# Softmax sums divided out in the output norm, and keys and queries squared from PSUM and normed at their one eviction

## What is computed

```python
k_sh = rms_norm((hk @ w_k).reshape(b, s, 8, 2, 64), k_norm_g)      # hk, h: normed residual stream
v_sh = (hk @ w_v).reshape(b, s, 8, 128)
q = rms_norm((h @ w_q[j]).reshape(b, s, 8, 2, 64), q_norm_g[j])
...
probs = softmax(where(causal, q . k * 64**-0.5, -1e30))            # two components per head
diff = probs[:, :, 0] - lam * probs[:, :, 1]
out = diff @ v                                                     # (queries, head, 128)
o = rms_norm(out, subln_g[j]) * (1.0 - lam_init)
x = x + o.reshape(b, s, 1024) @ w_o[j]
```

## Time and profile before

| | |
|---|---|
| time, median of 3 runs | 1270.95 us (1270.5 to 1271.31) |
| the profiled execution: its own time | 1270.56 us |
| its span from first to last instruction | 1268.7 us |
| mean granted TensorE clock over the span | 0.982 |
| TensorE, VectorE, ScalarE, GpSimd busy | 96%, 67%, 43%, 9% of the span |

### The profile page before, as it was taken

The page is one execution under the profiler, slowest core; times in us unless marked ns, Lnnn a source line. Parts: engine busy times, 40 slices in busy tenths (PEclk is TensorE's granted clock), DMA queues, the critical chain, the costliest instruction groups (busy, mean ns, idle before and its releaser), DMA issues.

```text
span 1268.7 us, 16583 instructions
## 1 busy us (share of the span) xinstructions
PE 1213.7 (96%) x6085; PEld 1014.2 (80%) x6085; DVE 843.9 (67%) x1158; ACT 542.1 (43%) x942; POOL 111.8 (9%) x99
## 2 busy tenths in 40 slices
PE   6998997999999999999998989987999999999999
PEld 4787765888888888887998989865888888888887
DVE  7999946577626763676677777664677537762673
ACT  6246966444313441344454545442544324431441
POOL 4000000200000000001234141301200000000000
PEclk9999998999999999999999999997999999999999
DMA  5221001323322223123221211211322322332222
GB/s 214 75 94 64 1 1 36 103 95 99 100 100 99 93 95 111 66 83 116 71 98 34 67 37 64 67 34 34 100 95 88 116 71 95 99 113 87 100 74 92
DMA packets 16615, 104.00 MB, mean 82 GB/s; under 512 B 1840, under 2 KB 1968, under 8 KB 5424
## 3 DMA queue, kind: packets, MB, share of 16 engines
q1 hardware_dynamic: 16560, 103.25, 24.5%
HBM read 101.15 MB, written 2.10 MB: 81 GB/s over the span
## 4 chain that ended last, share of the span: by engine, by line
PE 84%; DVE 10%; ACT 3%; POOL 1%; issue 1%; DMA 0%; SPq 0%; POOLq 0%; DVEq 0%; ACTq 0%
PE bank L1036 67%; PE bank L1154 7%; PE bank L1090 5%; PE bank L1219 2%; DVE prob L982 1%; DVE w_lo L709 1%; DVE small L972 1%; ACT prob L663 1%; DVE w_lo L701 1%; DVE prob L984 1%; POOL sq_sum L417 1%; DVE dT_lo L964 1%; PE bank L1107 1%; ACT w_hi L472 1%; PE bank L1188 1%
## 5 line engine op out<-in xcount | busy, mean ns | idle before, releaser
L1036 PE MATMUL bank<-xg_hi,w_hi 128*128 128x512 f32 x832 | 327.1, 393 | 13.3 <-DVE xg_lo L717 10.9
L1036 PE MATMUL bank<-xg_lo,w_hi 128*128 128x512 f32 x832 | 325.2, 391 | 0.0
L1036 PE MATMUL bank<-xg_hi,w_lo 128*128 128x512 f32 x832 | 325.0, 391 | 0.0
L472 ACT ACTIVATE w_hi<-w_raw 128x2048 fp32r<-128x2048 f32 x83 | 158.3, 1907 | 151.0 <-PE bank L1036 151.0
L701 DVE TENSOR_TENSOR w_lo<-w_raw,w_hi 128x2048 fp32r<-128x2048 f32 x83 | 192.6, 2321 | 30.9 <-ACT w_hi L472 30.9
L1036 PE MATMUL bank<-act_hi,w_hi 128*128 128x512 f32 x480 | 191.0, 398 | 9.0 <-DVE act_lo L833 7.2
L1036 PEld LDWEIGHTS bank<-xg_hi,w_hi 128*128 128x128 f32 x832 | 156.9, 189 | 48.2 <-DVE w_lo L732 10.8
L1036 PE MATMUL bank<-act_lo,w_hi 128*128 128x512 f32 x480 | 188.6, 393 | 0.0
L1036 PE MATMUL bank<-act_hi,w_lo 128*128 128x512 f32 x480 | 188.2, 392 | 0.0
L606 ACT ACTIVATE ffn_t<-ffn_u,par 128x512 f32<-128x512 f32 x88 | 72.0, 818 | 268.4 <-DVE ffn_u L886 268.4
L1036 PEld LDWEIGHTS bank<-xg_lo,w_hi 128*128 128x128 f32 x832 | 157.2, 189 | 33.1 <-issue 0.7
(11 more groups left out here) (141 smaller groups left out, 1563.4 us busy)
## 6 DMA issues: line engine op xcount, KB each, us to landing
w_raw<-stream SPq DMA_DIRECT2D x87, 1024.0 KB, 4.9
w_raw<-stream SPq DMA_DIRECT2D x8, 768.0 KB, 4.3
x<-x_t SPq DMA_DIRECT2D x8, 256.0 KB, 6.4
out_t<-x SPq DMA_DIRECT2D x8, 256.0 KB, 2.0
w_raw<-stream SPq DMA_DIRECT2D x2, 512.0 KB, 5.0
par<-params SPq DMA_DIRECT2D x1, 345.5 KB, 2.9
lam_in<-lambdas SPq DMA_DIRECT2D x1, 128.0 KB, 7.8
```

What stands on the lines that cost most here:

```text
L472: act.activation(w_hi[:, j, :], w_raw[:, j, :], ACT.Copy).then_inc(w_hi_done, 1)
L1036: got = pe.matmul(out, weights(w, j, k, m), v[:, k, :], start=(k == 0 and s == 0), stop=(k == count - 1 and s == 2), skip_group_check=True)
```

## The change

Softmax: the sums are no longer divided out of the blocks of `prob`. `differ` computes, for a whole set, the reciprocals `inv` and ratio = -lambda * inv1 * sum0, and combines e0 + ratio * e1 for each block. That is the old result times sum0, a factor of each query row. It is divided out behind the product with the values: ScalarE squares bank 7 with scale `inv` of component 0, and GpSimd multiplies the root by `inv` into `o_scale`, with which VectorE norms all four blocks in one operation. Keys and queries: ScalarE squares them straight from PSUM with scale `rs_t`, at the steps at which VectorE evicted them; GpSimd makes the root and multiplies it by `rs_t` (`kq_scale`, 128x16); VectorE then evicts each half bank with it at steps 13 (keys) and 19 (queries), and releases the banks there.

```diff
 pool, dense(g, q), odd steps, q halved:
-                if u < 2 and part % 2 == 1:
-                    kq = (k_sb, q_sb)[u][:, g % 2, part - 1:part + 1, :]
-                    pool.wait_ge(kqv_half, 6 * g + 2 * u + part // 2 + 1)
-                    if (g, u) > (0, 0):
-                        pool.wait_ge(kq_summed, 2 * g + u)
-                    pool.tensor_tensor(kq_sq[:, part - 1:part + 1, :], kq, kq, ALU.mult).then_inc(kq_squared, 1)
                 if q in (6, 9):
                     u = q // 8
                     pool.wait_ge(kq_summed, 2 * g + u + 1)
-                    own.wait(own.mark(pool.tensor_scalar(stat_in, stat, 1.0 / HD, EPS, ALU.mult, ALU.add)))
-                    own.wait(own.mark(power(stat_in, stat_in, [P, 4 * TB])))
-                    kq = (k_sb, q_sb)[u][:, g % 2, :, :].rearrange("p b (c d) -> p (b c) d", c=4)
-                    pool.tensor_tensor(kq, kq, stat_in.rearrange("p (a b) -> p a b", b=1).broadcast_to([P, 4 * TB, HD]),
-                                       ALU.mult).then_inc(kq_normed, 1)
+                    own.wait(own.mark(pool.tensor_scalar(kq_scale, stat, 1.0 / HD, EPS, ALU.mult, ALU.add)))
+                    own.wait(own.mark(power(kq_scale, kq_scale, [P, 4 * TB])))
+                    by_block = kq_scale.rearrange("p (b c) -> p b c", c=4)
+                    pool.tensor_tensor(by_block, by_block, rs_t.rearrange("p (b c) -> p b c", c=1).broadcast_to([P, TB, 4]),
+                                       ALU.mult).then_inc(kq_rooted, 1)
 pool, step(h, "output"):
-                    power(o_rs, o_in, [P, TB]).then_inc(o_root, 1)
+                    own.wait(own.mark(power(o_in, o_in, [P, TB])))
+                    pool.tensor_tensor(o_scale, o_in, inv[:, h % 2, :, 0], ALU.mult).then_inc(o_root, 1)
 act, dense(g, q):
+                if u < 2 and part % 2 == 1:
+                    act.wait_ge(tiles, TILE0 + 2 * n + part // 2 + 1)
+                    if (g, u, part) == (0, 0, 1):
+                        act.wait_ge(norm_rs, 3)
+                    if (g, u) > (0, 0):
+                        act.wait_ge(kq_summed, 2 * g + u)
+                    for b in (part - 1, part):
+                        got = act.activation(kq_sq[:, b, :], bank[2 * (n % RING) + part // 2][:, (b % 2) * 2 * P:(b % 2 + 1) * 2 * P],
+                                             ACT.Square, scale=rs_t[:, b:b + 1])
+                    got.then_inc(kq_squared, 1)
 act, step(h, "output"):
-                                             accum_out=o_ms[:, b:b + 1])
+                                             scale=inv[:, h % 2, b, 0:1], accum_out=o_ms[:, b:b + 1])
 dve, dense(g, q): the eviction of keys and queries at steps 3, 7, 11, 15 goes (values stay), and:
                 if q in (5, 8):
                     u = q // 8
                     dve.wait_ge(kq_squared, 4 * g + 2 * u + 2)
                     if (g, u) > (0, 0):
-                        dve.wait_ge(kq_normed, 2 * g + u)
+                        dve.wait_ge(kq_rooted, 2 * g + u)
                     dve.tensor_reduce(stat, ...).then_inc(kq_summed, 1)
+                if q in (6, 9):
+                    u = q // 8
+                    j = (FIRST["kqv"] + 3 * g + u) % RING
+                    dve.wait_ge(kq_rooted, 2 * g + u + 1)
+                    for half in range(2):
+                        to = (k_sb, q_sb)[u][:, g % 2, 2 * half:2 * half + 2, :].rearrange("p b (c d) -> p (b c) d", c=4)
+                        by = kq_scale[:, 2 * TB * half:2 * TB * (half + 1)].rearrange("p (a d) -> p a d", d=1)
+                        got = dve.tensor_tensor(to, bank[2 * j + half][:, :].rearrange("p (a d) -> p a d", d=HD),
+                                                by.broadcast_to([P, 2 * TB, HD]), ALU.mult)
+                    got.then_inc(kq_normed, 1)
+                    dve.wait_ge(kq_normed, 2 * g + u + 1)
+                    dve.sem_inc(banks_free, 1)
 dve, differ(h, n):
+                lo, hi = min(SETS[n]), max(SETS[n]) + 1
+                rows = slice(lo, hi, hi - 1 - lo if hi - lo > 1 else 1)
+                total = prob_sum.rearrange("p (b c) -> p b c", c=2)
+                own.wait(own.mark(dve.reciprocal(inv[:, h % 2, rows, :], total[:, rows, :])))
+                own.wait(own.mark(dve.scalar_tensor_tensor(out=ratio[:, rows], in0=inv[:, h % 2, rows, 1], scalar=neg_lam,
+                                                           in1=total[:, rows, 0], op0=ALU.mult, op1=ALU.mult)))
                 for b in SETS[n]:
-                    own.wait(own.mark(dve.reciprocal(inv[:, 2 * b:2 * b + 2], prob_sum[:, 2 * b:2 * b + 2])))
-                    own.wait(own.mark(dve.tensor_scalar(prob[:, n % 2, 1, w], prob[:, n % 2, 1, w],
-                                                        inv[:, 2 * b + 1:2 * b + 2], neg_lam, ALU.mult, ALU.mult)))
-                    dve.scalar_tensor_tensor(out=prob[:, n % 2, 0, w], in0=prob[:, n % 2, 0, w],
-                                             scalar=inv[:, 2 * b:2 * b + 1], in1=prob[:, n % 2, 1, w],
+                    dve.scalar_tensor_tensor(out=prob[:, n % 2, 0, w], in0=prob[:, n % 2, 1, w],
+                                             scalar=ratio[:, b:b + 1], in1=prob[:, n % 2, 0, w],
                                              op0=ALU.mult, op1=ALU.add).then_inc(d_done, 1)
 dve, step(h, "norm output"):
-                    for b in range(TB):
-                        got = dve.tensor_scalar(o_sb[:, b, :], bank[7][:, b * VD:(b + 1) * VD], o_rs[:, b:b + 1],
-                                                None, ALU.mult)
-                    got.then_inc(o_normed, 1)
+                    dve.tensor_tensor(o_sb[:, :, :], bank[7][:, :].rearrange("p (b d) -> p b d", d=VD),
+                                      o_scale.rearrange("p (b d) -> p b d", d=1).broadcast_to([P, TB, VD]),
+                                      ALU.mult).then_inc(o_normed, 1)
```

More of the change, by code:

```diff
@@ L200, in trunk @@
         mask16, at = put("mask16", at, [P, P], BF16)
-        small, at = put("small", at, [P, 112])
+        small, at = put("small", at, [P, 128])
         conv_area = -(-at // HOME) * HOME
@@ L216, in trunk @@
         prob_sum = small[:, 24:32]
-        inv = small[:, 32:40]
+        inv = small[:, 108:124].rearrange("p (h b c) -> p h b c", h=2, c=2)
+        ratio = small[:, 32:36]
         o_ms = small[:, 44:48]
         o_in = small[:, 48:52]
-        o_rs = small[:, 52:56]
+        o_scale = small[:, 52:56]
         half = small[:, 56:57]
         stat = small[:, 60:76]
-        stat_in = small[:, 76:92]
+        kq_scale = small[:, 76:92]
         sq, at = put("sq", area, [P, 2, SEQ])
@@ L323, in trunk @@
         y_s = sem("y_s")
-        kqv_half = sem("kqv_half")
+        v_half = sem("v_half")
         v_hi_s = sem("v_hi_s")
@@ L327, in trunk @@
         kq_summed = sem("kq_summed")
+        kq_rooted = sem("kq_rooted")
         kq_normed = sem("kq_normed")
@@ L430, in dense @@
                 q //= 2
-                u, part = divmod(q, 4)
-                if u < 2 and part % 2 == 1:
-                    kq = (k_sb, q_sb)[u][:, g % 2, part - 1:part + 1, :]
-                    pool.wait_ge(kqv_half, 6 * g + 2 * u + part // 2 + 1)
-                    if (g, u) > (0, 0):
-                        pool.wait_ge(kq_summed, 2 * g + u)
-                    pool.tensor_tensor(kq_sq[:, part - 1:part + 1, :], kq, kq, ALU.mult).then_inc(kq_squared, 1)
                 if q in (6, 9):
@@ L460, in _ @@
         def _(act):
-            places = iter(range(96, 112))
+            places = iter(range(92, 108))
             def fetch_table(function):
@@ L937, in dense @@
                         dve.wait_ge(v_hi_s, 2 * g + part // 2 + 1)
[L938 to L942, removed]
+                        for b in (part - 1, part):
+                            of = bank[2 * (n % RING) + part // 2][:, (b % 2) * 2 * P:(b % 2 + 1) * 2 * P]
                             got = dve.scalar_tensor_tensor(out=v_lo[:, g % 2, b, :], in0=of, scalar=rs_t[:, b:b + 1],
                                                            in1=v_hi[:, g % 2, b, :].bitcast(F32), op0=ALU.mult, op1=sub)
[L945 to L950, removed]
+                        got.then_inc(v_half, 1)
+                        if part == 3:
+                            dve.wait_ge(v_half, 2 * g + 2)
+                            dve.sem_inc(banks_free, 1)
                 if q in (5, 8):
```

## The result

The changed kernel takes 1274.66 us (median of 15 runs, 1272.34 to 1277.31), the kernel before 1270.62 us in the same number of runs: ratio 1.0036, 95% interval 1.0029 to 1.0043. It is slower by 0.36%, 4.0 us, where 1.9 us (1272.5) was forecast as the likeliest and the range went from 1266 to 1278. By the prediction's own line of 0.2% it is on the slower side, which had a chance of 0.32, and not among "same" with 0.48. The runs of the changed kernel also lie further apart: 5.0 us against 2.9.

The account below looks back on a forecast made before the run. TensorE's program order was taken to set the time. Terms +13.2 + 6.9 + 0.4 - 10.9 - 4.6 - 3.5 = +1.5 us on a profiled 1270.56, plus 0.4 for the median, gave 1272.5 us; range 1266 to 1278.

Parts of the forecast that it names:

- same: Outcome for the whole kernel: a time within 0.2% of the kernel before; chance 0.48.
- The order of the chain: Before score B, groups 1 to 3: VectorE's wait for the keys' root stalls TensorE 4.4 us each, 13.2 us.
- The clock: Behind each new stall before score B, TensorE's clock falls, costing 2.3 us three times, 6.9 us.
- The old waits: TensorE's nine `dT_lo` waits, 642 to 819 us: 10.9 us would go, with 0.4 us left in the third group.
- Up to turn Q of group 3: The attention stretch ahead of the tail: new stalls and clock loss against old waits and low clock removed.
- The tail: From 819 to 880 us, where a chain between engines is the limit: 3.5 us shorter.
- Contention: VectorE operations slowed beside GpSimd's keys and queries multiplications: 0.75 and 1.3 us regained, 3 to 4 us per group.
- s: Stall plus clock loss per new wait before score B, put at 6.7 us; net effect 3s - 18.6 us.
- B: From score B on, three groups: same wait, but clock low for longer; 1275.8 or 1279 us, chance 0.30.
- A: The forecast itself: the added wait about cancels what is won; 1271 to 1273.5 us, chance 0.46.
- C: Behind the stalls before score B: the clock isn't lowered; 1265.5 to 1269 us, chance 0.13.
- D: Before score B: VectorE's relief lands, wait hidden; 1252.4 us, or 1260 to 1267 if partly hidden; chance 0.11.

Follow-up runs that it names:

- e3: The changed kernel with the keys' root on GpSimd at step 11 instead of 13, ahead of the output's root; 1254.83 us.
- e2: The keys-and-queries part alone: the changed kernel with the old softmax combination, squares and output norm put back; 1278.20 us.
- e9: The changed kernel with 20 constant matmuls on TensorE ahead of its wait before score B of heads 1, 3 and 5; 1270.33 us.
- e6: e3 with VectorE evicting the queries ahead of the values at step 19 instead of behind them; 1252.00 us.
- e1: The softmax part alone: the kernel before with the new `differ`, scaled squares, `o_scale` and single norm operation; 1265.77 us.
- e7: e3 with an unneeded 128x1024 multiplication on GpSimd behind each root of keys or queries in groups 1 to 3; 1259.61 us.
- e11: e2 with the keys' root on GpSimd moved to step 11, as in e3; 1260.64 us.
- e10: e6 with 11, 14 and 6 constant matmuls in TensorE's three waits behind the last head; 1246.27 us.
- e5: The changed kernel with 36 constant matmuls on TensorE ahead of its wait before score B of heads 1, 3 and 5; 1279.34 us.
- e4: The changed kernel with GpSimd's order kept, but VectorE evicting the keys at step 15 instead of 13; 1264.48 us.
- e8: e6 with 24, 36 and 14 constant matmuls in TensorE's three waits behind the last head; 1254.08 us.

## Why the prediction came out as it did

- **The order of the chain**: right in every link, e3 proves the place. The wait before score B was to be 4.4 us and is 4.94. Evictions (1.29 + 0.15 us), small multiplications (0.20 and 0.23) and the root were as sized. The missing term is ScalarE's squares of the output: with `inv` as a scale per partition the four take 1.51 instead of 1.14 us. I had called them unchanged. In the trace of the changed kernel:

```profile
733.53 0.37 ACT L682 ACTIVATE o_sb<-bank,small 128x128 f32<-128x128 f32 x1 [2.33 <-PE bank L1234]
```

  In the old one, and in e2, it is 0.28 us. The Trainium skill's page ScalarE: Activation LUTs (What ACT_TABLE_LOAD costs) says that each pointer operand adds about 93 ns; the rows agree, with 0.37 against 0.28. Three times 0.37 us is 1.1 us of the 1.6 by which the waits came out longer.
- **The clock**: 6.9 us forecast, 6.3 by the windows, 1.8 for each wait by e9. Right.
- **The old waits**: 0.4 us was to be left and 3.5 is. This is the term that failed. The forecast had turn C in groups 1 and 2 right (0.33 and 0.35 us), but left the 0.4 for group 3 alone and put nothing at turn Q of groups 1 and 2, one step later. Behind the `dT_lo` for which turn C waits, VectorE still has two pairs of weight splits with `kT_lo` between them before the last `dT_lo` (in group 3 a whole-tile split and `kT_lo`), and TensorE waits 0.80 us in groups 1 and 2, and 1.25 in group 3, where it had waited 1.42 before. The query eviction of 1.28 us stands ahead of this stretch; e6 shows that it is part of the cause. Also, the operand for turn C came at 760.25 us, not at 758.0 to 758.6: the forecast let VectorE take the maxima of score B right behind combination A, but TensorE had only just been released and ran score B at the low clock:

```profile
746.18 1.42 DVE L985 TENSOR_REDUCE small<-bank 128x1 f32<-128x384 f32 x4 [1.04 <-PE bank L1207]
```

  So the margin of 2.0 to 2.6 us that the forecast had at turn C (TensorE there at 760.6) became a wait of 0.35, and the operand of turn Q, next on the same chain, was late as well. That all nine old waits would vanish without the added wait was wrong too: e3, which is that case, keeps 1.06, 0.80, 1.07, 0.80 and 1.33 us in groups 1 to 3.
- **Up to turn Q of group 3** the sum was +13.2 + 6.9 + 0.4 - 15.5 = +5.0 us; measured +7.0. The listed waits and low stretches would give 14.8 + 3.5 - 10.9 + 6.3 - 4.6 = +9.1. The other 2 us show when the 1611 matmuls of this stretch are laid side by side, start to start, in the two traces: the places of the waits make +6.0 and not +7.4, the low stretches +5.6 and -3.8, together +1.7, and the rest -0.7. The list counts a wait only from the end of the matmul before, 0.16 us after the next could have started, so the small waits at turn A and turn B of the old kernel (0.4 to 0.7 us in the list) were longer than listed; and at score C waits of 0.1 to 0.2 us, too short for the list, are gone. So the sum is off by only 2.0 us because a part of the errors, +1.6 for the stall, -0.6 for the clock and +3.1 for the old waits, was cancelled by this.
- **The tail**: -3.5 forecast, -2.4 measured. Head 6 gave 1.6 (2.0 forecast), head 7 1.0 (1.4), and behind the last output 0.2 came instead of 0.15 going, by the scaled squares again. Behind the tail 0.8 us were added, where the forecast had nothing; the clock stays low there for 2.3 us longer, which by the missing share is 1.1 us. The 1.3 us by which the change was early ahead of the attention is chance, and it hid as much.
- **Contention**: 1.3 us combinations and 2.4 us splits are gone as forecast, and e1 and e7 show from both sides that GpSimd was their cause.
- **The rivals**: s came to 4.9 + 2.1 = 7.0, just at the 7.1 that was named as the point from which B decides; the old waits that stayed did the rest. So 1274.66 us lies above A's own 1271 to 1273.5 and on B's side, but not for B's reason: the clock stayed low no longer than A had it, and the evictions took what A had put. C falls with the windows, and D needed the order that e3 made; e3 took 1254.83 where D had 1252.4. Of the signs named, the tail's "3 us or so" was missed with 2.4.

Open is why one wait of 2.75 us in e7 was followed by a low clock and the other was not, and why the 1.23 us in e11 was and the same wait in e2 was not.

## What to carry to other kernels

When a step moves from one engine to another, look up what stands ahead of it in the order of the engine that it now waits for, and what stands behind it on its own: the change lost 4 us with less work on the busiest helper, and moving one block two steps up in GpSimd's order made it a gain of 16. A wait of TensorE has two prices, its length and the clock behind it (here some 5 and 2 us), and both show in the windows; follow the new timeline until TensorE has passed the last operand of the stretch, not only the first. Where a wait can't be removed, matmuls on constants can keep the clock up (4.3 us in e9, 5.7 in e10), but only if they end before the wait does: overrunning cost its full length in e5. An operation on GpSimd that nobody waits for can still be on the path, through VectorE operations that run beside it.

## What the runs showed of the hardware

- A VectorE operation on one column (128x1, all operands in SBUF) took 1.68 us instead of 0.22 beside a GpSimd multiplication of SBUF tiles.
- Matmuls of 128x128 on plain float32 constants took 0.223 us each and stand as two in the trace; the output products on split operands take 0.11 us.
- TensorE waits of 2.0 us (e4, two of two) and 2.75 us (e7, one of two) were followed by a stretch at 1.2 GHz, and so was one of 1.23 us in e11 that came 3 and 5 us behind two others of 0.84 and 0.93. Waits of 1.42 us (before, e1) and 1.44 us (e4) were not, nor the 1.23 us in e2. Where the waits were filled with matmuls on constants (e5, e9, e8, e10), none was.
